# One core, two transformer blocks: key weights ahead of a modulation unit, a turn of query tokens moved up, rows outside in two pairs' down products

## What is computed

```python
def memory_cross_attention(xn, mn, w_xq, w_xkv, w_xo):
    q = (xn @ w_xq).reshape(B, S, XATTN_HEADS, XATTN_HEAD_DIM)
    k, v = jnp.split(mn @ w_xkv, 2, axis=-1)
    ...
ada = jax.nn.silu(c) @ w_ada[layer] + b_ada[layer]
ada_c = jax.nn.silu(c_ctx) @ w_ada[layer] + b_ada[layer]
...
# every expert e, on its own tokens
y = (silu(xe @ w1[e]) * (xe @ w3[e])) @ w2[e]
```

## Time and profile before

| | |
|---|---|
| median of 3 runs | 1299.24 us (1298.53 to 1300.81) |
| the profiled execution | 1300.37 us, span 1298.6 us |
| PE busy | 97% of the span |
| DVE, ACT, POOL busy | 54%, 39%, 8% |
| chain that ended last | PE 85%, DVE 7%, ACT 3%, issue 2%, DMA 1%, POOL 1% |
| DMA | 362.89 MB, mean 279 GB/s |

### The profile page before, as it was taken

How to read it: one execution, slowest core, us unless ns; L and a number is a source line. 1 busy time by engine, 2 the same in 40 slices (tenths; PEclk the granted TensorE clock), 3 DMA queues, 4 the chain that set the end, 5 groups by cost and what they waited for, 6 DMA issues and landing times.

```text
span 1298.6 us, 17828 instructions
## 1 busy us (share of the span) xinstructions
PE 1261.2 (97%) x7053; PEld 887.4 (68%) x7053; DVE 698.1 (54%) x1169; ACT 509.3 (39%) x778; POOL 102.9 (8%) x111
## 2 busy tenths in 40 slices
PE   8999999999999999999999999999999999999998
PEld 7987886976776444444445444449966787899986
DVE  5675668667664323322322222247996868855552
ACT  5556674345244111111111111137344685644442
POOL 6740200200000000000000000000043000000000
PEclk9999999999999999999999999999999999999999
DMA  9654747958876999999999999995416254655440
GB/s 350 240 193 140 251 151 262 371 180 292 308 283 238 402 424 426 426 427 428 429 428 427 425 429 427 427 397 199 154 65 221 104 201 140 194 167 169 184 162 33
DMA packets 103316, 362.89 MB, mean 279 GB/s; under 512 B 4306, under 2 KB 28373, under 8 KB 89600
## 3 DMA queue, kind: packets, MB, share of 16 engines
q1 hardware_dynamic: 99872, 352.60, 70.0%
q0 software_dynamic: 3168, 9.06, 2.2%
q10 hardware_dynamic: 192, 0.06, 0.0%
HBM read 360.65 MB, written 1.05 MB: 279 GB/s over the span
## 4 chain that ended last, share of the span: by engine, by line
PE 85%; DVE 7%; ACT 3%; issue 2%; DMA 1%; POOL 1%; ACTq 0%; DVEq 0%; POOLq 0%
PE bank L544 37%; PE bank L955 17%; PE bank L975 8%; PE bank L929 5%; PE bank L1330 5%; PE bank L1006 3%; DVE ring_parts L1378 2%; PE bank L965 1%; ACT ring_parts L2211 1%; DMA ring<-in_w_xkv 1%; PE bank L633 1%; PE bank L956 1%; PE bank L1170 1%; PE bank L598 1%; PE bank L831 1%
## 5 line engine op out<-in xcount | busy, mean ns | idle before, releaser
L1378 DVE TENSOR_TENSOR ring_parts<-ring,ring_parts 128x1024 fp32r<-128x1024 f32 x202 | 243.6, 1227 | 128.7 <-ACT ring_parts L2211 125.8
L2211 ACT ACTIVATE ring_parts<-ring 128x1024 fp32r<-128x1024 f32 x222 | 230.0, 1057 | 189.6 <-PE bank L544 164.7
L544 PE MATMUL bank<-ring_parts,arena_parts 128*128 128x512 f32 x1056 | 272.3, 393 | 4.1 <-ACT ring_parts L2211 1.5
L544 PEld LDWEIGHTS bank<-ring_parts,arena_parts 128*128 128x128 f32 x1056 | 196.6, 188 | 48.6 <-ACT ring_parts L2211 2.8
L544 PE MATMUL bank<-arena_parts,ring_parts 128*128 128x256 f32 x1504 | 199.4, 285 | 3.0 <-DVE ring_parts L1378 1.8
L955 PE MATMUL bank<-ring,arena 128*64 128x512 f32 x432 | 190.6, 594 | 8.2 <-issue 8.2
L956 PE MATMUL bank<-ring,arena 128*64 128x512 f32 x448 | 197.9, 595 | 0.0
L544 PEld LDWEIGHTS bank<-arena_parts,ring_parts 128*128 128x128 f32 x1504 | 191.4, 193 | 5.1 <-issue 3.3
L955 PEld LDWEIGHTS bank<-ring,arena 128*64 128x64 f32 x432 | 57.5, 137 | 126.7 <-issue 126.7
L2494 ACT ACTIVATE arena<-bank 128x512 f32<-128x512 f32 x32 | 19.1, 597 | 227.4 <-PE bank L956 227.4
L975 PE MATMUL bank<-ring,arena 128*64 128x512 f32 x416 | 106.3, 596 | 0.0
(11 more groups left out here) (411 smaller groups left out, 1502.1 us busy)
## 6 DMA issues: line engine op xcount, KB each, us to landing
ring<-in_w SPq DMA_DIRECT2D x70, 2048.0 KB, 20.9
ring<-in_w_in SPq DMA_DIRECT2D x27, 2048.0 KB, 9.7
ring<-in_w_ada SPq DMA_DIRECT2D x12, 2048.0 KB, 8.7
flank<-in_w SPq DMA_DIRECT2D x12, 2048.0 KB, 21.1
ring<-in_w SPq DMA_DIRECT2D x22, 1024.0 KB, 9.9
ring<-in_w_ffn_gate SPq DMA_DIRECT2D x11, 1024.0 KB, 5.3
ring<-in_w_ffn_up SPq DMA_DIRECT2D x11, 1024.0 KB, 8.0
ring<-in_w_ffn_down SPq DMA_DIRECT2D x5, 2048.0 KB, 7.7
```

Source lines behind the costliest of these rows:

```text
L544: mm = pe.matmul(ps[:, o:o + width], *pair, start=(o == 0 and kk == 0 and ha + hw == 0), stop=(kk == kn - 1 and (ha, hw) == terms[-1] and ...
L1378: dve.tensor_tensor(low, src, high, ALU.subtract).then_inc(low_ready, 1)
L2211: act.activation(high, src, ACT.Copy).then_inc(high_ready, 1)
```

## The change

It has three parts. Lines are numbered as in the kernel before.

First, the stage of keys and values: xkv0 is loaded ahead of ada3 (so xkv0 goes to slot 0 and ada3 to slot 1). PE does ada3 between xk0 and xk1 instead of before xk0, and the sums of ada2 and ada3 come after the first quarter of xk0 and xk1. DVE writes the first low part of xkv0 between the two tiles of the mix products, and the low activations of the other half before the ada sums. ACT copies two high parts of xkv0 before ada2's result, and ada3's after two quarters of xkv1. Second, PE turns the second tile of query tokens before ada6. Third, in the first two pairs of experts the down product has its rows of blocks outside (`down_by_rows`): each k is done for both halves of the output, and `half` is raised after k = 1, that is after 8 of 16 steps; both halves' results come complete with the last k.

```diff
-    ada_units(0, 4)
-    for j in range(4):
+    ada_units(0, 3)
+    whole("xkv0", cols(w["w_xkv"][0], 0))
+    ada_units(3, 4)
+    for j in range(1, 4):
         whole(f"xkv{j}", cols(w["w_xkv"][0], 512 * j))
...
             ada_part(2)
             ada_sum(1)
+            memory_arrived = halves_split(12)
+
+            def summed(j, arrived=None):
+                def between(q):
+                    if arrived is not None:
+                        arrived(q)
+                    if q == 1:
+                        ada_sum(j)
+                return between
+            split_features("xk0", "xkv0", mem_parts, summed(2, memory_arrived))
             ada_part(3)
-            ada_sum(2)
-            split_features("xk0", "xkv0", mem_parts, halves_split(12))
-            ada_sum(3)
-            split_features("xk1", "xkv1", mem_parts)
+            split_features("xk1", "xkv1", mem_parts, summed(3))
...
             ada_part(5)
+            turn(xT, hat2, hats=4, tiles_of=(1,))
             ada_part(6)
             ada_sum(4)
-            turn(xT, hat2, hats=4, tiles_of=(1,))
...
                 reach(pe, moe["hid"], 2 * n + 2)
+                if halved(n):
+                    down_by_rows(n, w2u)
+                    return
                 for half in range(2):
...
-                        if half and k == KF // 2 - 1 and halved(n):
+                    mm.then_inc(moe["down"], 1)
+
+            def down_by_rows(n, w2u):
+
+                for half in range(2):
+                    reach(pe, moe[f"low{half}"], n)
+                for k in range(KF):
+                    for half in range(2):
+                        for j in range(2):
+                            mm = pe.matmul(PS[4 + half][j * C:(j + 1) * C, :], hidT[:, j, k, :],
+                                           w2u[j][:, k, half * 512:(half + 1) * 512], start=(k == 0), stop=(k == KF - 1),
+                                           skip_group_check=True)
+                        if k == KF - 1:
+                            mm.then_inc(moe["down"], 1)
+                        elif half and k == KF // 2 - 1:
                             mm.then_inc(moe["half"], 1)
-                    mm.then_inc(moe["down"], 1)
...
+                if t == 0:
+                    split_low(1)
+
+            split_activations(mem_parts, actT, (1, 3))
             dve.wait_ge(s["G_ready"], 8)
             ada(0)
             ada(1)
-            split_low(1)
-            split_activations(mem_parts, actT, (1, 3))
...
             split_activations(memT, mem_parts, actT, (0, 2, 1, 3))
+            split_high(2)
             ada(2)
-            split_high(2)
+            split_high(4)
             ada(3)
-            split_high(2 + 12)
+            split_high(10)
```

## The result

The changed kernel takes 1306.30 us (median of 5 runs, 1305.55 to 1310.44); the kernel before, run beside it, 1300.33 us (5 runs, 1298.53 to 1300.81). The ratio is 1.0059 with a 95% interval of 1.004 to 1.0079: it is slower, by 6.0 us on the medians. The direction was forecast, and the size roughly (+4.4); the time lies 0.3 us above the top of the range.

A forecast was written before the change was run, and what follows sets the result against it. PE, busy 97% of the span, bounds the kernel, with loads setting the pace among the experts. Terms -0.9 + 1.85 + 0.44 + 3.0 + 1.5 + 0.3 - 1.8 = +4.4 on 1299.24 gave 1303.6 us, range 1300.0 to 1306.0.

The forecast's parts named there:

- the two waits: Keys and values: PE idles from 221.8 to 225.2 for bank 1 before xk0, and about 3 us for bank 0 before xv0.
- The start of xk0: Keys: xk0 starts at 225.2 instead of 226.11, held by DVE's late reading of bank 1; -0.9 us.
- The start of xv0: Values: PE stands until DVE copies xk0's first half out of bank 0; +3.0 us of new idle time.
- ada3 and the sum: Keys: ada3, no longer hidden under a load, adds +1.85 us; ada2's sum inside xk0 adds +0.44 us.
- The rival of the eight banks: Keys and values: both banks' readers end in time, no clock fall; -3.5 us, 1295.7 us, faster; chance 0.10.
- The rival in which the clock holds: Before xv0: stalls come but no clock loss follows; +2.1 us, 1301.4 us, within 0.2%; chance 0.22.
- the experts give nothing: Rival, experts: earlier half brings no gain, so the -1.8 us goes; +6.2 us, 1305.4 us; chance 0.14.
- The second fall of the clock: Values: the idle stretch ahead of xv0 likely brings the clock down again; +1.5 us.
- The turn: Queries: turning xT2 and xT3 before ada6 delays xq0 behind ACT's copy of ada6; +0.3 us, bounds -0.5 and +0.5.
- The experts: First pair's down product: earlier half fills a hole in the loads, shortening later load waits; -1.8 us, bounds -1.9 and 0.
- The term 0: Keys: the 1.7 us clock loss at xk0 stays as it is; 0, bounds -1.7 and +1.1.
- the forecast's own top: Upper end of the main forecast's own range, 1302.1 to 1305.1 us, all over 0.2% slower; forecast's chance 0.54.

The follow-up runs named there:

- e4: The changed kernel with DVE's program alone reordered, ada0's sum and second low part earlier, first key copies before xkv2's low parts: 1296.55 against 1300.14 us before.
- e5: The changed kernel with only DVE's early sum of ada0 and second low part before the low activations: 1302.44 against 1300.39 us for the kernel before.
- e6: The changed kernel with only the first key copies moved ahead of xkv2's low parts on DVE: 1301.28 against 1300.39 us for the kernel before.
- e10: The changed kernel run once more, unedited: 1306.74 against 1300.66 us for the kernel before, ratio 1.0051.
- e3: The kernel before with only the experts' part, down_by_rows in the first two pairs: 1298.72 against 1300.14 us.
- e2: The kernel before with only the turn of the second tile of query tokens moved ahead of ada6: 1302.49 against 1300.14 us.
- e9: The kernel before run once more, unedited, for its clock: 1300.49 us.
- e1: The kernel before with only the keys part of the change: 1308.84 against 1300.14 us.
- e11: The kernel before with the moved turn, ACT's high part of xT2 ahead of ada6's copy, and down_by_rows, keys as before: 1298.04 against 1300.66 us.

## Why the prediction was right and wrong

**Right, and shown by undoing it:** the two waits. The start of xk0 was put at 225.2 and came at 225.23; the cause was the reader of bank 1 (e4, e5), not a load. The start of xv0 was given +3.0 of idle time and had 3.05; the cause was the copy out of bank 0 (e6). With ada3 and the sum, +1.85 and +0.44, the terms up to xv0 make 4.39; measured 255.77 against 251.13, 4.64, since the second stall costs 3.2 us when it is counted from where xv0 would have started. The rival of the eight banks falls: in the trace PE waited 3.41 and 3.05 us at banks whose readers were late. The rival in which the clock holds falls too: ahead of xv0 it fell in all five executions that stood there, and ahead of xk0 it held in one of five (e10). That the experts give nothing is refuted by e3. The Trainium skill ("Perfetto Trace Analysis", section "Optimizing Tensor Performance") has matmul groups rotate through banks so that the reading of one overlaps the next group. This case shows what it needs besides: the reading must also stand early enough in the order of the engine that reads. With the same rotation and another order on DVE, e4 has neither wait.

**Right in sign, mis-sized:** small amounts, all in one direction. Up to xv0 it is 0.25 too little. The second fall of the clock was put at +1.5 and cost 1.57 (6.21 at ada4 less the 4.64 at xv0). The turn was put at +0.3, and e2 and the changed kernel show +0.48, near the upper bound. The experts were put at -1.8 and gave -1.47 in this profile. Together that is +0.8, from +4.4 to the +5.2 of the profile. The experts' share of it is hardly a mistake of the term: the eight profiles that show a gain have 1.3 to 2.0 at the last wait for loads, and e9 differs from the first profile of the same program by 0.27 there.

**Wrong:** the step that carried the profile over to the median. The sum was made against the profiled execution, 1300.37 us, with the fall behind xk0 left "as it is", and then added to the median, 1299.24, as if a program had its falls. The term 0 holds only against an execution that has that fall. Falls come and go between executions: of five with 1.8 to 2.0 us idle ahead of xk0 three had a fall there, of five with 3.4 us four, and all five with 3.05 us ahead of xv0; six had one of 1.5 to 1.7 us near 400 us or at 840 to 844 us, places for which the sum had no term. In the times of the kernel before the same is seen: of the 28 runs beside e1 to e4 the 12 with a mean granted clock of 0.999 or 1.000 took 1297.82 to 1299.74 us, the 16 with 0.996 to 0.998 took 1300.00 to 1303.26. By its time the 1299.24 us run, the middle one of three, belongs to the first sort (its clock was not recorded), and the profiled execution to the second. In the comparison the median of before was 1300.33: 1.1 us of the miss.

On the changed kernel's side it is the other way round. The mean granted clock of its five runs was 0.992 to 0.997; the two at 1309.59 and 1310.44 us have 0.995 and 0.992, the profiled one 0.996. So the median lies 0.75 us above the profiled execution. Where the falls of the 1309.59 and 1310.44 us runs lay was not recorded, and stays open. The 0.8 of the terms, this 0.75 and the 1.1 make up the 2.7 us from 1303.6 to 1306.30. A range drawn around the sum should have held one fall of 1.7 us more on its upper side. Its top of 1306.0 even lies below what the prediction's own upper bounds give together: 0.9 and 1.1 at xk0, 0.1 at xv0, 0.2 for the turn and 1.8 for the experts over the sum, 1307.7. (Two slips in the prediction change nothing: 1299.24 + 2.1 is 1301.3, not 1301.4, and 0.9 + 0.1 + 0.2 put the forecast's own top at 1304.8, not 1305.1.)

## What to carry to other kernels

When a product moves in a rotation of banks, write down for each of its banks who reads it last and what stands ahead of that reader in its engine's queue; here two reorderings on DVE, with no work added or taken away, turned +6 us into -3.6. A step that is moved earlier pays only if everything that it feeds moves too: the turn brought nothing until ACT's order followed it. Before a sum is compared with a median, look at how often the granted clock fell in the execution that the sum comes from, ask whether the runs of the median had the same falls, and leave room for one fall more or less.

## What the runs showed of the hardware

The clock's falls cost 1.3 to 1.7 us each in these traces; the cheapest, in the changed kernel, began at about 224.8, while PE still stood (xk0 starts at 225.23). They do not follow from the length of the idle time alone: 1.81 us (before) and 1.99 us (e2) ahead of xk0 came with one, 1.85 us (e3), 1.92 us (e11) and, in e10, 3.41 us did not; among the experts 2.26 us (e2) and 2.76 us (e11) did, 2.10 us (before) and 2.73 us (e9) did not; near 400 us it fell in e1 to e5, with no idle time over 0.6 us on PE from 380 us to there. What decides it, nothing here shows.
